# Low parts of the weights one row block later, the latent key rotated by GpSimd, and the first key product of the cross attention moved ahead of the mixer's output product

## The reference, cut to what matters

```
x = x + concat(mlstm heads * gates, memory_attention) @ w_out           # layer A
c_kv, k_pe = split(rmsnorm(x) @ w_kv_a, [256, 64])                      # layer B (latent keys)
k, v from rmsnorm(c_kv) @ w_kv_b ; k = rmsnorm(concat(k_nope, k_pe), k_gain)
k = concat(k[:128], rope(k[128:]))                                      # k_pe: all 8 heads share it
x = x + concat(chunk_causal_attention(q, k, v) * silu(z), memory_attention) @ w_out
u, q, k, v, gates = split(rmsnorm(x) @ w_in)                            # layer C (mixer)
x = x + (concat(pool(u), rmsnorm(diff_attention(q, k, v))) * sigmoid(gates)) @ w_out
k, v = split(rmsnorm(mem) @ w_ckv) ; q = rmsnorm(x) @ w_cq              # layer D (cross attention)
x = x + softmax(q k^T) v @ w_co
x = x + relu(rmsnorm(x) @ w_up)^2 @ w_down                              # layer E (MLP)
out = rmsnorm(x)
```

## Time and profile before

| | us |
|---|---|
| median of 3 runs | 1583.37 |
| lowest, highest | 1582.98, 1588.41 |
| the profiled execution | 1586.22 |
| its span in the profile | 1584.4 |
| TensorE busy | 1535.1 (97%) |
| VectorE busy | 887.2 (56%) |
| ScalarE busy | 707.6 (45%) |
| GpSimd busy | 223.0 (14%) |

### The profile page before, as it was taken

The page is one execution under the profiler, slowest core; times in us unless marked ns, Lnnn a source line. Parts: engine busy times, 40 slices in busy tenths (PEclk is TensorE's granted clock), DMA queues, the critical chain, the costliest instruction groups (busy, mean ns, idle before and its releaser), DMA issues.

```text
span 1584.4 us, 19220 instructions
## 1 busy us (share of the span) xinstructions
PE 1535.1 (97%) x7128; PEld 1245.0 (79%) x7128; DVE 887.2 (56%) x1747; ACT 707.6 (45%) x1611; POOL 223.0 (14%) x192
## 2 busy tenths in 40 slices
PE   7999999999999999999899999999999999999997
PEld 5887778887898777777588877788778888888886
DVE  6467485657465566666457567664446433444343
ACT  6554343334355767665334444443344423333241
POOL 3202020202120003222022005120002000000001
PEclk9999999999999999999999999999999999999998
DMA  6522122323424221112133221233232333333331
GB/s 193 160 67 80 53 81 67 94 67 120 119 74 142 81 61 55 52 57 67 41 120 100 87 67 54 67 116 111 93 93 68 107 100 100 93 94 106 94 94 66
DMA packets 89069, 141.04 MB, mean 89 GB/s; under 512 B 6417, under 2 KB 36497, under 8 KB 88977
## 3 DMA queue, kind: packets, MB, share of 16 engines
q1 hardware_dynamic: 88256, 139.02, 28.8%
q10 hardware_dynamic: 720, 0.81, 0.2%
HBM read 137.71 MB, written 2.10 MB: 88 GB/s over the span
## 4 chain that ended last, share of the span: by engine, by line
PE 78%; DVE 9%; ACT 5%; issue 3%; POOL 3%; DMA 2%; SPq 0%; POOLq 0%; ACTq 0%; DVEq 0%
PE banks L1246 16%; PE banks L1248 16%; PE banks L1247 16%; PE banks L1251 6%; PE banks L1253 6%; PE banks L1252 6%; DVE sb_w_split L1938 2%; PE banks L1209 2%; DVE sb_arena L1947 2%; ACT sb_junk L1517 2%; PE banks L1372 1%; ACT sb_w_split L1549 1%; PE banks L1425 1%; PE banks L1488 1%; DVE sb_arena L1941 1%
## 5 line engine op out<-in xcount | busy, mean ns | idle before, releaser
L1938 DVE TENSOR_TENSOR sb_w_split<-sb_raw,sb_w_split 128x512 fp32r<-128x512 f32 (+4 forms) x530 | 344.4, 692 | 365.5 <-ACT sb_w_split L1549 364.8
L1549 ACT ACTIVATE sb_w_split<-sb_raw 128x512 fp32r<-128x512 f32 (+4 forms) x530 | 288.1, 592 | 424.3 <-PE banks L1248 307.7
L1246 PE MATMUL banks<-sb_actA,sb_w_split 128*128 128x512 f32 x672 | 276.4, 411 | 2.4 <-DVE sb_arena L1938 2.1
L1248 PE MATMUL banks<-sb_actA,sb_w_split 128*128 128x512 f32 x672 | 263.1, 392 | 0.0
L1247 PE MATMUL banks<-sb_actA,sb_w_split 128*128 128x512 f32 x672 | 262.1, 390 | 0.0
L1246 PE MATMUL banks<-sb_actB,sb_w_split 128*128 128x512 f32 (+1 forms) x640 | 248.5, 388 | 1.5 <-DVE sb_actB L1938 1.5
L1248 PE MATMUL banks<-sb_actB,sb_w_split 128*128 128x512 f32 (+1 forms) x640 | 242.9, 380 | 0.0
L1247 PE MATMUL banks<-sb_actB,sb_w_split 128*128 128x512 f32 (+1 forms) x640 | 242.6, 379 | 0.0
L1251 PE MATMUL banks<-sb_w_split,sb_actA 128*128 128x512 f32 (+1 forms) x384 | 153.7, 400 | 13.3 <-DVE sb_w_split L1938 9.9
L2458 POOL TENSOR_TENSOR sb_arena<-sb_arena 128x512 f32<-128x512 f32 x43 | 63.4, 1474 | 686.5 <-ACT sb_arena L1590 684.1
L1246 PEld LDWEIGHTS banks<-sb_actA,sb_w_split 128*128 128x128 f32 x672 | 126.5, 188 | 32.3 <-issue 7.2
(11 more groups left out here) (217 smaller groups left out, 2084.7 us busy)
## 6 DMA issues: line engine op xcount, KB each, us to landing
sb_raw<-in_a_w_in SPq DMA_DIRECT2D x66, 256.0 KB, 3.0
sb_raw<-in_w_up SPq DMA_DIRECT2D x32, 512.0 KB, 3.7
sb_raw<-in_w_down SPq DMA_DIRECT2D x32, 512.0 KB, 3.8
sb_raw<-in_w_in SPq DMA_DIRECT2D x24, 512.0 KB, 3.6
sb_raw<-in_mem_w_kv SPq DMA_DIRECT2D x16, 512.0 KB, 3.8
sb_raw<-in_w_ckv SPq DMA_DIRECT2D x16, 512.0 KB, 3.7
sb_raw<-in_a_w_in SPq DMA_DIRECT2D x15, 512.0 KB, 3.8
sb_raw<-in_a_w_out SPq DMA_DIRECT2D x12, 512.0 KB, 3.8
```

Source lines behind the costliest of these rows:

```text
L1246: pe.op.matmul(out, hi[:, cs], x.hi(k), start=i == 0, stop=False)
L1248: t = pe.op.matmul(out, lo[:, cs], x.hi(k), start=False, stop=last_i)
L1549: act.op.activation(hi[:, cs], raw[:, cs], ACT.Copy).then_inc(act.mark(m("w_hi"), 2 * n + part + 1), 1)
L1938: dve.op.tensor_tensor(out, a, b, op).then_inc(dve.mark(*mark) if mark else dve.tick(), 1)
```

## The change

1. The step `split` keeps ScalarE's half; VectorE's half becomes a step `low`. `product()` holds it back until the next `step()`, so it is put after half a chunk (one row block) instead of next to the split. In products with fewer than 512 tokens it is put at once.
2. `kpe` moves from VectorE's program to GpSimd's: one product with the gain of 128x256 in place of four of 128x64, then the six of the rope.
3. In the closing list of a head `dho` comes one group later.
4. Product ckD0 is placed ahead of outC0; its evictions wait for the memory's norm and the last pooling step. ckD1 takes ckD0's old place after outC1, and cqD0 and cqD1 follow each other. The buffers of the queries and of the keys change places in the arena, since the pooling still uses the old place.

```diff
     def step(self):
+        self.low()
         if self.soon:
...
+    def low(self):
+        if self.held_low is not None:
+            self.put(("low", self.held_low))
+            self.held_low = None
...
+                self.low()
                 self.put(("split", self.n_split))
+                self.held_low = self.n_split
+                if pr.tokens < SEQ:
+                    self.low()
...
-                closing.append([[("dhs", h)], [("dhr", h)], [("dho", h)], [("ysplit", "yC", 4 + h)]])
+                closing.append([[("dhs", h)], [("dhr", h)], [], [("dho", h)], [("ysplit", "yC", 4 + h)]])
...
+    p.product("ckD0", [("nrow", "m2"), ("pw", POOL_GROUPS - 1)])
     p.product("outC0", first=False)
     p.product("outC1")
...
-    p.product("ckD0")
+    p.product("ckD1")
     p.rings = [(4, 5), (6, 7)]
     for g in range(2):
-        p.product(f"cqD{g}", [("nrow", "d")], first=False)
-        if g == 0:
-            p.product("ckD1")
+        p.product(f"cqD{g}", [("nrow", "d")], first=g > 0)
...
+        self.cqT = at.take(8, SEQ)
         self.ckT = at.take(KD, N_MEM)
         self.cv = at.take(MT, D_MODEL)
-        self.cqT = at.take(8, SEQ)
...
-        if kind == "split":
+        if kind == "low":
...
+        elif kind == "kpe":
...
+            tensor(g, v.ckv[:, :, KV_LORA:320], gain.unsqueeze(1).broadcast_to([P, TT, QK_ROPE]), ALU.mult)
+            pool.settle()
+            pool.wait_ge(*m.at("cos", ("rotab2",)))
+            s1, s2, o1, o2 = g[:, :, 0:HALF], g[:, :, HALF:], v.kpe[:, :, 0:HALF], v.kpe[:, :, HALF:]
+            tensor(o1, s1, v.cosB, ALU.mult)
+            tensor(tmp, s2, v.sinB, ALU.mult)
+            pool.settle()
+            tensor(o1, o1, tmp, ALU.subtract)
+            tensor(o2, s2, v.cosB, ALU.mult)
+            pool.settle()
+            tensor(tmp, s1, v.sinB, ALU.mult)
+            pool.settle()
+            tensor(o2, o2, tmp, ALU.add, *m.at("kpe", step))
```

More of the change, by code:

```diff
@@ L478, in finish @@
         total = len(self.chunks)
-        self.order = [s for s in self.order if s[0] not in ("split", "fetch") or s[1] < total]
+        self.order = [s for s in self.order if s[0] not in ("split", "low", "fetch") or s[1] < total]
         self.chunk_of = {c: n for n, c in enumerate(self.chunks)}
@@ L545, in order_of_work @@
     p.put(("split", 0))
+    p.put(("low", 0))
     p.put(("fetch", 2))
@@ L549, in order_of_work @@
     p.put(("split", 1))
+    p.put(("low", 1))
     p.n_split, p.n_fetch = 2, 3
@@ L711, in order_of_work @@
     turned, closing = None, []
-    for n in range(len(units) + 8):
+    for n in range(len(units) + 9):
         group, after, split = [], [("rtp", "q", 3)] if n == 0 else [], []
@@ L1908, in evict_waits @@
         return [m.product("mv1")]
+    if name == "ckD0":
+        return [m.at("pooled", ("pw", POOL_GROUPS - 1))]
     if name == "uC":
@@ L2281, in vector_program @@
             second_part(step, v.src[src], k, v.col("kv_lat_norm" if src == "latT" else "q_lat_norm", k))
[L2282 to L2291, removed]
         elif kind.startswith("prep"):
@@ L2482, in gpsimd_program @@
             pool.op.tensor_tensor(u[:, 0:16], edge, u[:, 0:16], ALU.subtract).then_inc(pool.mark(*m.at("pooled", step)), 1)
+        elif kind == "kpe":
+            g = v.prob[:, 0, 0:TT * QK_ROPE].rearrange("p (i n) -> p i n", i=TT)
+            tmp = v.prob[:, 1, 0:TT * HALF].rearrange("p (i n) -> p i n", i=TT)
+            gain = v.rows[:, ROW["k_gain_pe"]:ROW["k_gain_pe"] + QK_ROPE]
+            pool.wait_ge(m("dma_params"), 48)
+            for i in range(TT):
+                pool.wait_ge(*m.evicted("ckvB", i))
+            pool.settle()
[10 more added lines that the diff above has]
+            tensor(tmp, s1, v.sinB, ALU.mult)
+            pool.settle()
+            tensor(o2, o2, tmp, ALU.add, *m.at("kpe", step))
         elif kind in ("prep4", "prep5"):
```

## The result

The changed kernel takes 1589.97 us (median of 22 runs, 1583.9 to 1595.0) against 1585.01 for the kernel before (22 runs, 1582.93 to 1589.63): ratio 1.0027, 95% interval 1.0018 to 1.0036. By the ratio it is slower by some 4.3 us, where a gain of 4.5 us was forecast, and its time lies outside the range. The profiled execution took 1588.83 us, its span is 1586.0, the mean granted clock 0.992 (before 0.994).

What follows compares the result with a forecast made beforehand. TensorE's rows of matmuls, 78% of the chain, were taken to set the time. Terms -2.3 + 0.9 - 0.9 - 1.3 - 0.9 = -4.5 us, from 1583.37 to 1578.9; range 1571.5 to 1586.5.

Steps and rivals of the forecast that it cites:

- the first term: First layer, 134 to 142: low part put behind the row maximum; -1.28, clock -1.6, give-back +0.6, sum -2.3 us.
- GpSimd holds VectorE: Rival, chance 0.14: the latent key's rotation on GpSimd costs VectorE 4.4 instead of 0.7 us; total -0.8, so 1582.6 us.
- My two signs of being wrong: TensorE waiting for weights' low parts behind 100 us, or ScalarE's idle time for transfers growing by more than 3 us.
- The rule: Rotation on GpSimd: by the shared-port lock VectorE could lose the full 4.4 us, making the edit +2.4 us.
- The one at 636.45: A fused two-operand 128x512 VectorE instruction, 0.69 us inside six GpSimd instructions; cited against the full 4.4 us loss.
- a stall of 1.70: First layer, near 141: TensorE's remaining stall, 2.98 - 1.28, taken as harmless to the clock, so 1.6 us counted as won.
- The start of the second layer: 467 to 480: a ckvB low part ends some 2.7 us later and delays a fetch; +0.9 us, between 0 and +2.7.
- The rival of starved fetches: Rival, chance 0.10: late low parts hold fetches at three places, 8.1 in place of 0.9; total +2.7, 1586.1 us.
- The rotation with its neighbours: Latent key's rotation to GpSimd: stalls at 558.89 and 564.17 go, -2.0; contention +0.7; sum -1.3 us.
- The z blocks: Blocks zB1 to zB3: normalisations no longer behind low parts; -0.35, -0.55 and 0, so -0.9 us, between 0 and -2.5.
- Mixer and ckD0: Third head's stall in the mixer shrinks from 2.27 to about 1.4, -0.9 us; ckD0 ahead of outC0 taken at 0.

Runs made afterwards that it cites:

- the reordering alone: The kernel before with only ckD0 ahead of outC0, the head's output transposes a group later, and cqD0 and cqD1 together; ratio 1.0001 to the kernel before.
- the early rotation: Changed kernel with layer A's low parts next to their split and GpSimd's rotation right behind the cosines; ratio 0.9989 to the kernel before.
- the kernel with layer A at once: Changed kernel with the low parts of layer A's products put next to their split again; ratio 0.9995 to the kernel before.

## Why the prediction was wrong

**The step that failed** is the first term, "give back 0.6 for the second eviction, which now stands behind the moved low part", with its sum of -2.3. It measured +5.1. Two errors are in it. I gave the moved low part its undisturbed 1.29 us, though it lands beside GpSimd's SiLU product: the two halves in fact take 3.08. The earlier trace rows had shown a low half of 1.52 us under GpSimd, and I weighed it for the rotation only. The earlier trace rows had it at this very place: two low parts at 1.29 are 2.6 us, and the row says 4.29. Low halves and GpSimd in the kernel before, 134 to 139:

```profile
L1938 DVE TENSOR_TENSOR sb_w_split<-sb_raw,sb_w_split x4: 679/1128/1590, 134.1 to 137.7; 128x512 fp32r<-128x512 f32 x4
...
133.99 1.12 POOL L2547 TENSOR_TENSOR sb_arena<-sb_arena 128x512 f32<-128x512 f32 x1 [1.95 <-ACT sb_arena L1718]
135.20 1.42 POOL L2549 TENSOR_TENSOR sb_arena<-sb_arena 128x512 f32<-128x512 f32 x1
```

Chunk 25's halves took 1.6 us each beside GpSimd, chunk 26's 0.7 behind it; the change moved chunk 26's to the next SiLU product. And I worked out head 0 alone, where heads 1 and 2 repeat it; they are 4 of the 5.1 us. The mechanism of my rival "GpSimd holds VectorE" decided, in another place than I put it. My two signs of being wrong looked at late weights, not at this meeting, and neither came up: behind 100 us TensorE waits once for a low part, 0.41 us at 495.56 (before twice, 0.63 in all).

**The rule** that the prediction names (the Trainium skill, SBUF — State Buffer, section "SBUF: two separate sides"), by which a VectorE instruction with two SBUF inputs and a GpSimd instruction that reads SBUF lock each other out, was priced for the rotation alone. This case's rows agree with it for layer A: the two halves of chunk 26's low part end behind GpSimd's two instructions, and the instruction with an operand in the banks did not wait (0.41 against 0.87 and 1.15). The one at 636.45 that was not slowed, my reason against the rule, is no counterexample: it started first, 0.06 us ahead of GpSimd's fourth, and it was this one that grew, to 1.23 us, where the other five took 0.74 to 1.05. GpSimd's fourth by itself:

```profile
636.51 1.23 POOL L2441 TENSOR_TENSOR sb_arena<-sb_arena 128x256 f32<-128x256 f32 x1
```

**The clock.** To call a stall of 1.70 harmless as "below the 2.14 that did no harm" took one draw for a threshold. The stall of the last transposes of outB, 2.15 or 2.16 us in all 13 profiles, was followed by a clock of 0.5 in ten of them, the kernel before among them (778.21, granted 0.72 from 778 to 784), and not in three (the changed kernel, the reordering alone, the early rotation). Before the query product the clock fell in all six profiles of the new order with that stall (2.0 to 2.3 us) and in none of the three of the old order; why the order matters is open.

**The other terms.** The start of the second layer: +0.9 forecast, 0.1 measured (outA1 to mk1); ScalarE's wait for that transfer is 1.82 us after, not longer than the 4.05 before. The rival of starved fetches, nearest in its number, did not happen, so that its nearness is luck: ScalarE's waits for weight transfers sum to 53 us before and after. The rotation with its neighbours: -1.3 forecast, -1.3 measured, though the first unit's stall grew by 1.1 and not by 0.7 us. The z blocks: -0.9 forecast, -2.3 measured to zB3, since all three gave; some of it returns as a stall of 1.29 at 727.34, where 0.20 stood. Mixer and ckD0: -0.9 and 0 forecast, +1.3 measured: the head's stall only changed its name, and the query product lost 1.7 to the clock. Of the 11 us between 1578.9 and 1589.97, 1.6 lie in the base: the median of the kernel before was 1583.37 in 3 runs and is 1585.01 in 22.

Of the 4.3 us the profiled pair shows 2.6 (1588.83 - 1586.22). The clock can account for the whole: its mean over the 22 executions of the changed kernel is 0.9911, over the 97 of the kernel before that ran beside the experiments 0.9934 to 0.9941, and 0.0023 to 0.0030 of 1586 us are 3.6 to 4.8 us (estimate). At a like clock the two kernels would take about the same time by this: what layer A loses in stalls layer B wins back, and the loss is in clock falls behind the new stalls. In the profiled execution they come at 145, 237, 558 and 1077, and in the one before at 141 and 780; of layer A's 5.1 us, head 1's is 1.7.

## What to carry to other kernels

Moving an instruction later on its engine means asking two things of the new place: who stands behind it in the queue, and what the neighbour engine does at that moment; its duration is to be read from rows beside that neighbour, not from rows at rest. A merged row that is longer than its count times the price at rest says that the neighbour is already there. Look at every repetition of the pattern, not at the first. An instruction of GpSimd that is needed later can be held behind VectorE's urgent one by a single wait: here one wait took the kernel with layer A at once from 0.9995 to 0.9979 of the time before (the intervals overlap a little), while in the kernel before the same wait could not be told from no change.

## What was not expected of the hardware

The granted clock falls behind the same stall in some executions and not in others, and one fall costs nearly as much as the stall: 1.7 us in the 5 us behind a stall of 2.2. It also fell behind stalls as short as 1.0 to 1.3 us, in kC (823 to 848), in seven of the eleven profiles that have one of that length. So an edit of some tenths of a microsecond can't be judged from one profiled execution here.
